# Forgetting attention, row blocks taken widest, narrowest, third, second within each head pair

## The reference

```python
q_blocks = q.reshape(B, n_qb, Q_BLOCK, FOX_HEADS, FOX_HD).transpose(1, 0, 3, 2, 4)
def one_block(args):                    # Q_BLOCK = 128 rows of queries
    qb, cb, pos = args
    s = jnp.einsum("bhqd,bhkd->bhqk", qb, kh).astype(jnp.float32) * scale
    s = s + cb[..., :, None] - c[:, :, None, :]
    s = jnp.where(pos[:, None] >= k_pos[None, :], s, NEG_INF)
    p = jax.nn.softmax(s, axis=-1)
    return jnp.einsum("bhqk,bhkd->bhqd", p.astype(vh.dtype), vh)
```

## Time and profile before

| | |
|---|---|
| time, median of 3 runs | 2936.34 us (2936.06, 2936.34, 2945.63) |
| time of the profiled execution | 2939.83 us |
| span of the profiled execution | 2938.2 us |
| TensorE busy | 2828.8 us, 96% of the span |
| VectorE / ScalarE / GpSimd busy | 1587.3 / 990.5 / 200.4 us |
| share of the chain that ended last: PE / DVE / ACT | 90% / 5% / 3% |
| attention stage | 731.45 to 780.27 us, 48.82 us |

### The profile page before, as it was taken

One profiled execution on the slowest core, in us unless ns is written; L12 is line 12 of the kernel. 1 busy time (PEld: TensorE's weight loads), 2 busy tenths in 40 slices (PEclk: granted clock), 3 DMA queues, 4 the chain that ended last, 5 costly groups with the idle time before them and its releaser, 6 DMA issues.

```text
span 2938.2 us, 45465 instructions
## 1 busy us (share of the span) xinstructions
PE 2828.8 (96%) x19385; PEld 2348.5 (80%) x19385; DVE 1587.3 (54%) x2309; ACT 990.5 (34%) x1346; POOL 200.4 (7%) x251
## 2 busy tenths in 40 slices
PE   8989999999999999999999999998989999999998
PEld 6778888898788888778878788887778778888887
DVE  5658777845577777465343553334564343543334
ACT  5643222335532222433333332222533332331223
POOL 4100000000000000020040000000020030000000
PEclk9999999999999999799999999999989999999999
DMA  4334555521145554210023232232220013233222
GB/s 149 101 102 133 178 169 166 155 72 44 51 129 184 167 175 147 61 58 11 3 76 93 94 100 92 95 101 66 72 67 3 17 58 101 87 99 101 95 92 71
DMA packets 238530, 281.94 MB, mean 96 GB/s; under 512 B 7444, under 2 KB 224856, under 8 KB 238344
## 3 DMA queue, kind: packets, MB, share of 16 engines
q1 hardware_dynamic: 225312, 227.07, 24.3%
q0 software_dynamic: 12896, 52.11, 6.0%
q10 hardware_dynamic: 136, 0.03, 0.0%
HBM read 277.09 MB, written 2.10 MB: 95 GB/s over the span
## 4 chain that ended last, share of the span: by engine, by line
PE 90%; DVE 5%; ACT 3%; issue 1%; DMA 0%; ACTq 0%; POOL 0%; DVEq 0%; POOLq 0%
PE psum L2372 25%; PE psum L2373 24%; PE psum L2374 24%; PE psum L2874 1%; PE psum L2860 1%; PE psum L2420 1%; ACT whi L838 1%; PE psum L2421 1%; PE psum L2422 1%; DVE wlo L1508 1%; PE psum L2844 1%; PE psum L2459 1%; PE psum L2772 1%; PE psum L2796 1%; PE psum L2810 1%
## 5 line engine op out<-in xcount | busy, mean ns | idle before, releaser
L1508 DVE TENSOR_TENSOR wlo<-raw,whi 128x2048 fp32r<-128x2048 f32 x222 | 517.7, 2332 | 533.0 <-ACT whi L838 532.4
L2372 PE MATMUL psum<-hh,whi 128*128 128x512 f32 x1976 | 783.0, 396 | 13.7 <-DVE hl L1548 6.6
L2373 PE MATMUL psum<-hl,whi 128*128 128x512 f32 x1976 | 776.5, 393 | 0.0
L2374 PE MATMUL psum<-hh,wlo 128*128 128x512 f32 x1976 | 775.7, 393 | 0.0
L838 ACT ACTIVATE whi<-raw 128x2048 fp32r<-128x2048 f32 x222 | 423.8, 1909 | 552.4 <-PE psum L2374 552.4
L2372 PE MATMUL psum<-mh,whi 128*128 128x512 f32 (+1 forms) x1248 | 485.6, 389 | 4.2 <-issue 2.3
L2373 PE MATMUL psum<-ml,whi 128*128 128x512 f32 (+1 forms) x1248 | 479.3, 384 | 0.0
L2374 PE MATMUL psum<-mh,wlo 128*128 128x512 f32 (+1 forms) x1248 | 479.0, 384 | 0.0
L2372 PEld LDWEIGHTS psum<-hh,whi 128*128 128x128 f32 x1976 | 375.8, 190 | 99.7 <-issue 18.6
L2374 PEld LDWEIGHTS psum<-hh,wlo 128*128 128x128 f32 x1976 | 375.3, 190 | 79.1
L2373 PEld LDWEIGHTS psum<-hl,whi 128*128 128x128 f32 x1976 | 375.7, 190 | 78.2 <-issue 1.0
(11 more groups left out here) (451 smaller groups left out, 2960.7 us busy)
## 6 DMA issues: line engine op xcount, KB each, us to landing
rest<-in_ada_w POOLq DMA_DIRECT2D x64, 768.0 KB, 5.3
raw<-in_w_gu SPq DMA_DIRECT2D x44, 1024.0 KB, 5.1
raw<-in_w_in SPq DMA_DIRECT2D x34, 1024.0 KB, 5.2
raw<-in_w_mlp_in SPq DMA_DIRECT2D x32, 1024.0 KB, 5.4
raw<-in_w_mlp_out SPq DMA_DIRECT2D x32, 1024.0 KB, 5.2
raw<-in_w_out SPq DMA_DIRECT2D x16, 1024.0 KB, 5.3
raw<-in_w_down SPq DMA_DIRECT2D x16, 1024.0 KB, 5.3
raw<-in_w_mem_kv SPq DMA_DIRECT2D x8, 1024.0 KB, 5.3
```

Source lines behind the costliest of these rows:

```text
L1508: ins = dve.tensor_tensor(wlo[:, g % 2, :, :], raw[:, g % 2, :, :], f32(whi[:, g % 2, :, :]), ALU.subtract)
L2372: pe.matmul(out, whi_, xhi, start=first, stop=False)
L2373: pe.matmul(out, whi_, xlo, start=False, stop=False)
L2374: return pe.matmul(out, wlo_, xhi, start=False, stop=last)
```

## The change

The order of the four row blocks within each head pair is taken from a table instead of being t = j mod 4: the widths go 4, 1, 3, 2 instead of 1, 2, 3, 4. Every function that derives t or the width from the unit's number does it through the table; job numbers, steps, waits, buffers and counts of instructions stay.

```diff
+BLOCK_ORDER = (3, 0, 2, 1)
                             if j < PAIRS:
-                                n = P * (j % NT + 1)
+                                n = P * (BLOCK_ORDER[j % NT] + 1)
...
                             if 2 <= j < PAIRS + 2:
-                                n = P * ((j - 2) % NT + 1)
+                                n = P * (BLOCK_ORDER[(j - 2) % NT] + 1)
...
                             if j >= 4:
-                                b, h, t = J["fox_o", l, j - 4], (j - 4) // NT, (j - 4) % NT
+                                b, h, t = J["fox_o", l, j - 4], (j - 4) // NT, BLOCK_ORDER[(j - 4) % NT]
...
                     def fox_scores(j):
 
-                        h, t = j // NT, j % NT
+                        h, t = j // NT, BLOCK_ORDER[j % NT]
...
-                        for k in range(j % NT + 1):
+                        for k in range(BLOCK_ORDER[j % NT] + 1):
                             ins = pe.transpose(p[:, k * P:(k + 1) * P], f_p[:, (2 * j + i) % 6, k * P:(k + 1) * P], ident[:, :])
```

More of the change, by code:

```diff
@@ L1891, in fox @@
                             if 1 <= j < PAIRS + 1:
-                                n = P * ((j - 1) % NT + 1)
+                                n = P * (BLOCK_ORDER[(j - 1) % NT] + 1)
                                 for i in range(2):
```

## The result

| | before | changed |
|---|---|---|
| median of 20 runs | 2944.90 us (2936.06 to 2950.48) | 2946.61 us (2942.23 to 2958.96) |
| ratio of the changed kernel to before | | 1.0016, 95% interval 1.0008 to 1.0023 |
| profiled execution | 2939.83 us | 2950.11 us |
| its span | 2938.2 us | 2948.5 us |
| attention stage in it | 48.82 us | 52.07 us |

A forecast was written before the change was run, and what follows sets the result against it. TensorE bounds the kernel, and in the attention stage only its waits can move: full rounds +4.2, drain -1.5, fill +0.1, together +2.8 us with one clock fall again. From 2936.34 that gives 2939.1 us, range 2935 to 2948.

The forecast's parts named there:

- The race between the chain and TensorE's cover: Each attention step: TensorE waits where the serial VectorE and ScalarE chain outlasts its own work; full rounds +4.2 us.
- behind S1: Steps 5, 9, 13, after the scores of width 1: T waits 1.52 us, a gap of some 1.35.
- behind S2: Steps 7, 11, 15, after the scores of width 2: T waits 0.90 us, a gap of some 0.75.
- behind S3 or S4: Remaining full-round steps, after the scores of widths 3 and 4: no wait, or 0.1 us after width 4.
- Fill: First steps of the stage, up to the T of step 5: 1.3 us lost against 1.2 before, difference +0.1.
- drain: Last steps, without new scores: waits of 1.64 us shrink to 0.1 or 0.2 in all, difference -1.5.
- The sum at full clock: Whole attention stage at the high clock: full rounds, drain and fill together +2.8 us.
- I take one fall again: TensorE's clock in the stage: one fall to 1.2 GHz as before, priced 2.74 us; none or two kept as ends.
- more falls: Rival, clock in the stage: three or four falls in place of one, +6.5 to +8.3 us, about 2943 to 2945; chance 0.14.
- no change: Verdict on the whole kernel: same 0.97, faster 0.01, slower 0.02, with a bound of 0.5%, 14.7 us.
- The level: Whole kernel: forecast median 2939.1 us, from a base of 2936.34, the median of the three runs shown.
- The rival that the alternation pays: Attention stage: alternating wide and narrow evens ScalarE's load and removes waits, -4.5 to -7.2 us, 2929 to 2932; chance 0.12.

The follow-up runs named there:

- Cutting the chain: Instructions H (ScalarE) and M (VectorE) moved to the head of each step in the changed kernel: stage 45.05 us, ratio to the kernel before 0.9984.
- the filled kernel: Kernel before, with mask matmuls repeated 5 times from step 5 on to keep TensorE busy in its gaps: stage 46.15 us, run once, 2933.25 us.
- H moved: Only ScalarE's H at the head of the step: changed order stage 43.33 us, ratio to the kernel before 0.9976; old order 45.21 us, 0.9979.
- H and M first in the old order: H (ScalarE) and M (VectorE) at the head of each step in the kernel before: stage 44.89 us, ratio 1.0000.

## Why the prediction was right or wrong

**The race between the chain and TensorE's cover: right.** Both kinds of gap came where they were forecast, and as large: 1.35 forecast and 1.39 or 1.40 measured behind S1, 0.75 forecast and 0.75 and 0.76 measured behind S2 where the clock was up. No gap came behind S3 or S4. Cutting the chain took away every wait of T for M.

**Fill and drain: right in the main.** The first V waited 0.69, where about 1 was forecast, and nothing in the drain showed a wait for another engine. The sum at full clock was 2.8; 2.65 was measured.

**"I take one fall again": wrong.** There were three and two. The reason given held (a slow stretch does lengthen TensorE's cover: the gap behind S2 shrank from 0.75 to 0.45, 0.36 and 0.21), but the next 1.4 us gap comes four steps later and the clock could fall again there. What it did to the difference is small, because the kernel before also had a second fall in its other profile, in the drain: falls cost 3.27 and 3.67 us in the changed kernel (52.07 and 52.47 less 48.80) and 2.67 and 3.91 in the one before (48.82 and 50.06 less 46.15). The unit of price was wrong too: not the fall counts but the time at 1.2 GHz, some 10 us in three of these four profiles and 7 in the first of the kernel before, at 0.32 to 0.39 us lost for each. The three falls of the changed kernel took 10 us together, the one fall on which the prediction was made took 7. For that fall its price of 2.74 was right (2.67 by the filled kernel), but the falls of the changed kernel were half as long. So the rival "more falls" named the mechanism and put its price too high: 2.74 for each fall, where 3.27 / 3 = 1.1 was measured.

**The total: sign and size of the sum right, the verdict of "no change" right only by the 0.5% bound.** Measured +4.7 (2.4 to 6.8), forecast +2.8, the stage in two pairs of profiles +3.3 and +2.4. Whether the 1.9 us between 2.8 and 4.7 is anything is not settled: it is inside the interval and smaller than the scatter of the rest of the span. The rest was longer in the changed kernel in both pairs of profiles, by 7.0 and 2.4 us, so something outside of the stage isn't ruled out; but with the stage back at 48.80 us the same order was timed at 0.9995, and no run shows another place where the change would act.

**The level: wrong by the base, and this is the step that failed.** "Forecast for the median: 2936.34 + 2.8" took the median of three runs for what the kernel before takes. 2936.34 was the low end of that (20 runs 2944.90; later sets of 23 to 31 runs 2940.81 to 2942.55); two of the three are the lowest of the twenty. The base was 8.6 low, and the 2939.1 built on it lies 5.8 under the kernel before, so read as a time it says faster where slower was measured. The text saw 2945.63 among the three and set the range by it, but kept the median as its base.

**The rival that the alternation pays: wrong here, and right in part with H moved.** With the chain as it was the order cost 2.65 us; with H first its stage was 1.9 us the shorter one, 0.6 to 0.8 of it at full clock. Most of the 4.5 to 7.2 us that the rival hoped for came with H and in both orders. It had been argued against with the serial chain, which is what the runs show.

**What stays open:** why H and M first in the old order was timed at 1.0000 (0.9990 to 1.0010) when its stage was 3.9 us shorter. Its one profiled execution was 2935.94 us, its rest of the span 2889.4, as the kernel before. 0.9990 would be 2.9 us. The granted clocks of the single executions give a lead. The profiled one had 0.976 over its whole span, but its ten runs together 0.9715 and the 31 runs of the kernel before beside them 0.9722, although 7 to 10 us less at 1.2 GHz in the stage should by itself raise it by 0.0012 to 0.0017. Over those 31 runs an execution is 1.9 us longer for each 0.001 of clock less, so the missing 0.002 is worth some 4 us, an estimate: the clock was down for longer elsewhere in the program. Why, no run shows.

## What to carry to other kernels

In a hand-written software pipeline, price one step as a race: the serial chain that frees a buffer (every instruction that stands ahead of the releaser on its engine, whoever it belongs to) against what the waiting engine has to do meanwhile. Balance over steps says nothing; look at which wide item meets which narrow cover. Before reordering the work, move the releasing instruction ahead of what it doesn't need: here one instruction of 0.29 us, moved on ScalarE, took 3.6 us off the stage in the old order and 8.7 in the changed one, falls of the clock included (about 2.1 and 5.5 at full clock); no change of the order alone took off as much. And take a base from many runs where scatter (here 14 us between the ends of 20) is larger than the change.

## What the runs showed of the hardware

A gap of TensorE of 1.34 to 1.40 us was followed by a stretch at 1.2 GHz in seven of eleven cases (five of six in the two profiles of the changed kernel, two of four in those of the kernel before, not behind the 1.35 in the drain with H and M first in the old order). Shorter gaps give no sure rule either. Of 1.04 to 1.11 one of nine was: none of the five in the order 1, 4, 2, 3, and one of the four in the drain of the old order. Of 0.68 to 0.76 two of twelve were: the 0.71 in the fill of the order 1, 4, 2, 3, and one of two of 0.72 with H moved in the old order. None of 0.38 was. Every stretch in the stage lasted 3.4 or 6.8 us, to the 0.1 us that the windows view gives. Filling a gap with matmuls that do nothing new made the stage 2.7 and 3.3 us shorter, though TensorE did more work. The Trainium skill ("TensorE: Matmul & The Clock Gate", "A second HAM failure mode: psum-queue depth-cycling") says that frequent short idles of TensorE between groups of matmuls, in a kernel that cycles through PSUM banks, make the clock oscillate; the changed kernel's three falls in one stage agree, with 3.3 us for the three.
